# Filling two DRAM buffers with zeros: 31 transfers spread over the dense feed-forward stage, or three long ones issued in attention

## The reference, cut to what matters

```python
h = h + mla(rms_norm(h, g0), ...)                     # 8 heads, causal, rotary part shared
h = h + swiglu(rms_norm(h, g1), w_gate, w_up, w_down) # D_FF_DENSE = 2688
h = h + multiscale_pool(rms_norm(h, g2), ...)
logits = (xf @ router); top_v, top_i = lax.top_k(logits, 2)
dest = pad_start[sorted_e] + rank                     # rows are sorted by expert, each expert padded
xb = xf[buf_tok]                                      # gathered rows
yb = lax.map(expert_block, (xb, block_e))             # swiglu per block with its expert's weights
y = zeros.at[buf_tok].add(yb * buf_gate[:, None])
return rms_norm(h + y, final_norm)
```

## Time and profile before

| | |
|---|---|
| median of 3 runs | 1165.39 us |
| the profiled execution, its own time | 1164.74 us |
| its span in the profile | 1163.2 us |
| TensorE, busy | 1098.0 us |
| VectorE, busy | 381.5 us |
| ScalarE, busy | 278.1 us |
| GpSimd, busy | 63.0 us |
| moved by the DMA engines | 225.31 MB |

### The profile page before, as it was taken

How to read it: one execution, slowest core, us unless ns; L and a number is a source line. 1 busy time by engine, 2 the same in 40 slices (tenths; PEclk the granted TensorE clock), 3 DMA queues, 4 the chain that set the end, 5 groups by cost and what they waited for, 6 DMA issues and landing times.

```text
span 1163.2 us, 19082 instructions
## 1 busy us (share of the span) xinstructions
PE 1098.0 (94%) x7414; PEld 997.9 (86%) x7414; DVE 381.5 (33%) x703; ACT 278.1 (24%) x533; POOL 63.0 (5%) x128
## 2 busy tenths in 40 slices
PE   5999999999999999999987999999999999999980
PEld 4878887888888888888777899999999999999980
DVE  5585673543444334443664010010101010101015
ACT  5445552332422224222340001010101010101011
POOL 2200000000000000000002000000000000000003
PEclk9999999999999999999998999999999999999995
DMA  7031316163537445372305999999999999999986
GB/s 259 6 89 43 119 37 199 38 188 114 167 95 230 120 132 146 103 218 66 92 18 206 284 262 273 268 281 299 285 300 284 302 282 304 281 302 287 298 233 239
DMA packets 272654, 225.31 MB, mean 194 GB/s; under 512 B 29372, under 2 KB 245436, under 8 KB 272624
## 3 DMA queue, kind: packets, MB, share of 16 engines
q1 hardware_dynamic: 260192, 185.88, 56.9%
q0 software_dynamic: 11040, 36.36, 9.7%
q10 hardware_dynamic: 1392, 2.64, 0.7%
HBM read 198.43 MB, written 26.43 MB: 193 GB/s over the span
## 4 chain that ended last, share of the span: by engine, by line
PE 87%; DVE 6%; DMA 3%; ACT 1%; issue 1%; SPq 0%; POOL 0%; ACTq 0%; POOLq 0%; DVEq 0%
PE bank L1315 26%; PE bank L1329 14%; PE bank L917 13%; PE bank L919 13%; PE bank L918 13%; PE bank L1089 1%; PE bank L1376 1%; PE bank L929 1%; DMA stage_own<-in_moe_w_down 1%; PE bank L1069 1%; DMA stage_own<-in_moe_w_gate 1%; PE bank L1080 1%; PE bank L1304 1%; PE bank L1219 1%; DVE w_lo L1402 1%
## 5 line engine op out<-in xcount | busy, mean ns | idle before, releaser
L1315 PE MATMUL bank<-scratch,stage_own 128*128 128x128 f32 (+1 forms) x2720 | 327.9, 278 | 6.6 <-DMA stage_own<-in_moe_w_up 2.4
L1315 PEld LDWEIGHTS bank<-scratch,stage_own 128*128 128x128 f32 x2720 | 318.2, 191 | 8.8 <-DMA stage_own<-in_moe_w_up 2.6
L1833 DVE TENSOR_TENSOR qr_now<-krT,bank 128x128 f32<-128x128 f32 (+1 forms) x80 | 23.3, 292 | 377.1 <-ACT krT L867 377.1
L1329 PE MATMUL bank<-qr_now,stage_own 128*128 128x128 f32 (+1 forms) x1152 | 143.7, 278 | 0.2 <-DMA stage_own<-in_moe_w_down 0.2
L1329 PEld LDWEIGHTS bank<-qr_now,stage_own 128*128 128x128 f32 x1152 | 137.3, 191 | 0.6 <-DMA stage_own<-in_moe_w_down 0.6
L917 PE MATMUL bank<-big_hi,w_lo 128*128 128x512 f32 (+2 forms) x352 | 134.4, 382 | 0.0
L919 PE MATMUL bank<-big_hi,w_hi 128*128 128x512 f32 (+2 forms) x352 | 134.3, 381 | 0.0
L918 PE MATMUL bank<-big_lo,w_hi 128*128 128x512 f32 (+2 forms) x352 | 134.2, 381 | 0.0
L867 ACT ACTIVATE krT<-bank 128x128 f32<-128x128 f32 (+1 forms) x80 | 22.4, 280 | 375.4 <-PE bank L1315 369.1
L1402 DVE TENSOR_TENSOR w_lo<-stage_own,w_hi 128x1024 fp32r<-128x1024 f32 (+1 forms) x91 | 105.4, 1202 | 13.4 <-ACT w_hi L619 13.3
L619 ACT CAST w_hi<-stage_own 128x1024 fp32r<-128x1024 f32 (+1 forms) x91 | 88.9, 1032 | 14.2 <-DMA stage_own<-in_mla_w_down 6.3
(11 more groups left out here) (244 smaller groups left out, 1130.6 us busy)
## 6 DMA issues: line engine op xcount, KB each, us to landing
stage_own<-in_moe_w_gate SPq DMA_DIRECT2D x82, 512.0 KB, 5.6
stage_own<-in_moe_w_up SPq DMA_DIRECT2D x82, 512.0 KB, 5.9
stage_own<-in_moe_w_down SPq DMA_DIRECT2D x72, 512.0 KB, 4.6
stage_own<-in_ffn_w_gate SPq DMA_DIRECT2D x21, 512.0 KB, 6.0
stage_own<-in_ffn_w_up SPq DMA_DIRECT2D x21, 512.0 KB, 7.3
stage_own<-in_ffn_w_down SPq DMA_DIRECT2D x21, 512.0 KB, 4.5
xbuf<-scratch POOLq DMA_DIRECT2D x21, 496.0 KB, 6.4
scratch<-xbuf POOLq DMA_DIRECT2D x9, 576.0 KB, 6.4
```

The source lines that it names most:

```text
L1315: last = t_.matmul(dst[:, 0:n], w[:, k * P:(k + 1) * P], xT[:, k, 0:n], start=k == 0, stop=k == KD - 1)
L1329: last = t_.matmul(bank[4 + k // 3][:, col:col + n], w[0:parts, k * P:(k + 1) * P], e_act[0:parts, par, 0:n], start=first and k % 3 == 0, ...
L1833: v.tensor_tensor(e_act[:, par, 0:n], e_silu[:, par, 0:n], bank[2 * par + 1][:, 0:n], ALU.mult).then_inc(prod_ready, 1)
```

## The change: what it does

The 31 transfers of the FFN stage go. In their place GpSimd issues three transfers, two for `xbuf` (1296 rows each) and one for `ybuf` (its rows from 1152 to 2303). They come ahead of the wait for the last head and behind a new wait, for the unit `pair, 1, 1` in `weight_lo`, the 14th. The source is no longer a 4 KB row of `scratch`. It is the constant tile `zeros` (128 columns of float32, 512 bytes in each partition), of which 72 partitions are read, and each of them over and over: 144 times for a transfer to `xbuf`, 128 times for the one to `ybuf`. So one transfer has 72 x 144 = 10,368 pieces of 512 bytes, and the three have 29,952.

`xbuf` has 2592 rows in place of 2604. The clearing of `zero_rows` is gone, with its two waits, and ACT's wait for `zero_stored` before the norm is gone. The wait at the scatter stays, for 48 in place of 496.

```diff
-XZERO = -(-(JMAX + 2) * C // (FI * FG))
-XROWS = FI * FG * XZERO
-YPIECES = 2 * (FI - 2)
-YZERO = -(-(JMAX - E) * C // YPIECES)
+XROWS = (JMAX + 2) * C
...
+            pool.wait_ge(weight_lo, plan.unit("pair", 1, 1) + 1)
+            half = (JMAX + 2) // 2 * C
+            for rows in (xbuf[0:half, :], xbuf[half:, :], ybuf[E * C:, :]):
+                pool.dma_start(rows.rearrange("(p r) (c n) -> p (r c) n", p=ZP, n=P),
+                               zeros[0:ZP, :].unsqueeze(1).broadcast_to([ZP, rows.shape[0] // ZP * (D // P), P])
+                               ).then_inc(zero_stored, 16)
+
             pool.wait_ge(pv_done, H)
...
-            pool.wait_ge(xnT_done, 2 * T)
-            g.memset(zero_rows, 0.0).then_inc(zeros_ready, 1)
-            pool.wait_ge(zeros_ready, 1)
-            for i in range(FI):
-                for j in range(FG):
-                    if j == 0:
-                        pool.wait_ge(prod_ready, i * FG + 2)
-                    elif j == 2 and i < FI - 1:
-                        pool.wait_ge(h_ffn, i * 8 + 4)
-                    at = (i * FG + j) * XZERO
-                    pool.dma_start(xbuf[at:at + XZERO, :], zero_rows[0:XZERO, :]).then_inc(zero_stored, 16)
-                for n in range(2 * i, min(2 * i + 2, YPIECES)):
-                    at = JMAX * C - (n + 1) * YZERO
-                    pool.dma_start(ybuf[at:at + YZERO, :], zero_rows[0:YZERO, :]).then_inc(zero_stored, 16)
...
-            pool.wait_ge(zero_stored, 16 * (FI * FG + YPIECES))
+            pool.wait_ge(zero_stored, 48)
...
-            act.wait_ge(zero_stored, 16 * (FI * FG + YPIECES))
             for t in range(T):
                 act.wait_ge(h_ffn, 8 * (FI - 1) + 4 + t + 1)
```

More of the change, by code:

```diff
@@ L219, in trunk @@
         xn = view(0, T * D, T)
-        zero_rows = scratch[:, 0:D]
         cn = view(5120, 1792, 2)
@@ L272, in trunk @@
         zero_stored = sem("zero_stored")
-        zeros_ready = sem("zeros_ready")
         scattered = sem("scattered")
```

## The result

| | before | after |
|---|---|---|
| median | 1165.11 us (4 runs, 1164.74 to 1168.94) | 1182.18 us (4 runs, 1180.36 to 1184.30) |
| profiled execution, its span | 1163.2 us | 1182.5 us |

The changed kernel is slower by 17 us: the ratio is 1.014, with an interval of 1.0111 to 1.0168. I had forecast no change, 1165.2 us in a range of 1161.5 to 1174. That was wrong. The profiled execution of the changed kernel took 1184.12 us, so it has about 2 us more than the median to explain.

A forecast was written before the change was run, and what follows sets the result against it. TensorE bounds the kernel (busy 1098.0 of 1163.2 us), the DMA engines the experts. All terms 0: 1163.2 + 0, with 1.54 us outside 1164.7; median 0.65 us above that run: 1165.2 us, no change, range 1161.5 to 1174.

The forecast's parts named there:

- The start: GpSimd in attention: the first transfer is issued at 84.8 us, after the 14th count of `weight_lo`.
- GpSimd's writing: GpSimd in attention: issuing the three transfers takes 15 to 27 us, far end 127, under 109 us of cover.
- Gain of the removed work: FFN stage: removing 31 transfers, about 50 us of DMA time within 340 us of unbroken TensorE work, gains 0.
- The weights of the later pairs: Attention, loads beside the fill: they land in time, cost 0, bounds 0 and 5 us; late-weights rival 1168 us, chance 0.03.
- DMA share up from 0.20 to about 0.7: Sign that the forecast is right: DMA share of 84.9 to 182.5 us, falling back by about 155 us.
- What they cost the DMA engines: Fill in attention: 15.34 MB takes 49.4 us on sixteen engines, at the slow pace 73.8; with loads it ends at 153.5.
- my reading of q0's packets: GpSimd's queue, first 20 us: 160 packets mean pieces are packed up to 4 KB, so zeros move at earlier zero stores' pace.
- what shares the engines with the fill: Attention: next pairs' loads have 21.3 us of cover; at 8.7 us per weight load both land by about 98 us.
- the step on strict turns: Attention: if engines alternate one 4 KB fill packet with one 512-byte load piece, the first load lands at 100 us, in time.
- The fill or its instructions last too long: Rival, slower: the gain load stands behind the fill and decides if it ends after about 198 us; 1174 us, chance 0.05.
- DVE is held up: Rival, slower: GpSimd's writing of pieces delays DVE's scaling of probabilities in attention, 10 to 23 us; 1182 us, chance 0.12.
- the slow end of my fill: Attention: at the slower DMA pace the fill ends at 177.9 us, before `x` is read again at 182.47.

The follow-up runs named there:

- e1_ffn_place: Kernel after the change, but the same three transfers are issued in the FFN stage (about 232 us) instead of in attention: 1178.54 us, ratio 1.0096.
- e7_tiny: As e1_ffn_place, plus the same three transfers in attention with only 16 bytes of each 512-byte piece: 1186.59 us, ratio 1.0182.
- f2_ffn_p64: As e1_ffn_place (fill in the FFN stage), but each transfer reads 64 partitions: 1183.13 us, ratio 1.0140.
- f3_ffn_4k_apart: As e6_ffn_4k, but GpSimd waits for each transfer before it issues the next: 1181.19 us, ratio 1.0130.
- e6_ffn_4k: As e1_ffn_place with 72 partitions, but pieces are 4 KB rows of cleared scratch, and ACT waits for the fill again: 1218.89 us, ratio 1.0447.

## Why the prediction was wrong

**Held.** The start (84.93 us for 84.8). GpSimd's writing: 4.27 + 4.20 + 3.79 = 12.3 us, a little under the low end of 15. Gain of the removed work: 0 in the FFN, at 340 us of busy TensorE. ACT's dropped wait: 0. The weights of the later pairs: no wait of ACT's casts for `stage_own` between 84 and 200 us, though a load of `wo` now lands in 11.8 us for 4.4.

**Held by luck.** The sign "DMA share up from 0.20 to about 0.7" came out at 0.68. I had put the whole fill on all engines into that stretch. What moved there is 188 GB/s x 97.6 us = 18.3 MB, of which 6.3 were loads, so about 12 of the fill's 15.34 MB, on fewer engines for the whole time. TensorE was busy 93.87 us there, not 95 to 96.

**Failed: "What they cost the DMA engines".** The step took the pace of zero stores from 124 partitions in 4 KB pieces, 78.3 us of one engine for 1.52 MB, and divided by sixteen. That is 51.5 us a MB; the change ran at 69.3, on 77% of the engines. At the pace of the 15 us in which it ran alone (2.67 MB) the whole fill would take 86 us in place of my 49.4 (an estimate), and with the loads it took 135. In its place the runs give three factors. The piece: 1.26 (33 to 41.7 us a transfer at 72 partitions), or 1.16 in engine time if 59.6 us a MB from 128 partitions is set against my 51.5. So my reading of q0's packets was wrong as to their price: a packet of eight pieces costs more than one of 4 KB. As to their number it was right from 64 and 128 partitions (4.1 KB a packet). From 72 there are, besides, 432 packets under 512 B among the 1081, which I can't explain. The partitions: 41.2 us between the first two issues against 25.5 with 128, a factor of 1.6. 108 partitions (77% of the engines, quick pieces) and 64 (all engines, slow pieces) both lie at 34.3, so each of the two ways in which 72 partitions are bad is worth about 1.35 by itself here. This factor decides: with 128 partitions and all else the same the time is 1167, not 1182 us. And the loads meanwhile, which I had added as 19.3 us of all engines; from 182 us on those of `x` and the FFN came on top.

The Trainium skill, DMA: Bandwidth & Descriptors, section on why a DMA increments its semaphore by 16, gives 12 engines for 72 partitions, and 12 for 108, 16 for 64 and 128. The shares of 0.771, 0.773, 0.989 and 0.996 agree (12 of 16 is 0.75). My ground for setting the rule aside was slices of 0.8 and 0.9 with three transfers of 124 partitions in flight. It may stand for those, but it said nothing of 72, and carrying it over was the error. The slow pieces have a rule too: the Trainium skill, SBUF — State Buffer, section Door 1, says that the speed of a DMA depends on how many of 16 ports its partitions reach. By its formula 64 partitions reach 8 ports, 72 reach 10, and 96, 108 and 128 reach all. The slow pieces at 64 and 72 and the quick ones at 96, 108 and 128 agree with it in direction. The size is not that of the ports alone: half of them made the pieces 1.4 times as dear (83.6 against 59.6 us a MB).

**Failed beside it: what shares the engines with the fill.** I priced a load beside the fill by rows 13, 8.7 us to land. In the FFN stage SP stood at a single load for 19.6 us (e1_ffn_place), 25.7 (e7_tiny), 20.9 (f2_ffn_p64), 18.4 (f3_ffn_4k_apart) and 34.2 (e6_ffn_4k). After the change itself the longest was 10.2 us, and the four loads of `x` took 13.9. I had the mechanism in the step on strict turns, and used it only to show that the first pair's weights would make it, which they did.

**The rivals.** "The fill or its instructions last too long" named the place, the gain load behind the fill, and the point from which it decides, a fill that ends after 198 us. It ended at 220, and this rival is what came true, at about twice its size (17 us for 9). I gave it 0.05, since I took 12 engines at the slow pace as its far end (202.5 us). "DVE is held up" exists: two of 32 scalings stood 2.3 and 3.5 us, and the profiled execution is 2.6 us late behind them. Its 1182 us was the measured time, for the wrong reason: I let every transfer cost a head, and the first fell between two scalings. The Trainium skill, SBUF — State Buffer, section on the two sides, describes this lock for a whole instruction; the ends at 130.38 and 173.22 us against 130.33 and 173.16 agree.

**The bounds.** Even the slow end of my fill (177.9 us) was too short by 42 us, because both ends came from rows with 124 or 128 partitions, and the loads that share the engines after 182 us were left out. The partitions of the source were in the diff, and no row of the trace showed a long transfer from 72. A bound for that was missing.

## What to carry to other kernels

A long transfer is not free because the DMA engines are idle on the mean: ask how many partitions its SBUF side spans, and what another queue needs while it runs. Here 128 in place of 72 partitions was the difference between 17 us and nothing. A long backlog in one queue can starve another queue's loads (34.2 us at one load with 15 MB waiting), so short transfers tied to the work's rounds, as before the change, are the safer choice, and whatever is needed soon must not stand behind them in the same queue. Keep GpSimd's transfers of thousands of pieces away from a DVE that scales in SBUF on the critical chain.

## What the hardware showed that I had not expected

- An issue from GpSimd of 10,368 pieces takes 4.3 us on 72 or 108 partitions and 3.3 to 3.5 us on 64, 96 or 128. The next one waits until most of the first is served (37 us at 72 partitions), while two of 5184 go out together.
- Larger pieces helped the transfer (33 for 41.7 us) and did not help the others: with three such transfers waiting, TensorE stood 49.5 us for weights.
- An issue can hold SP or ACT for long: 19.6 us for SP, 18.5 and 18.1 us for ACT.
- Left open: why the same fill in the FFN stage held TensorE 17.7 us in one kernel and 6.5 us in another, what the packets under 512 B from 72 and 108 partitions are, and where 3.7 us of the expert stage came from.
